# A two-layer decoder step on one core: score products of 64 rows in two banks, normalized queries stored once, down rows of the experts requested early, norms and vector work reordered

## The reference: what is computed

```
def layer_forward(x, c, ...):
    sh1, sc1, gt1, sh2, sc2, gt2 = split(silu(c) @ w_ada + b_ada, 6)
    h = rms_norm(x, g_mix) * (1 + sc1) + sh1
    q, k, v, u, g = in_proj(h, w_in, ...)     # q, k: 4 heads x 2 maps x 64, rms-normed per map
    o = attend(q, k, v, lam)                  # softmax(map 0) - lam * softmax(map 1), times v
    o = rms_norm(o, subln) * (1 - lambda_init)
    y_pool = pool_mix(u, ...)                 # trailing windows 2, 4, 8, 16
    merged = g0 * (o @ w_branch[:512]) + g1 * (y_pool @ w_branch[512:])
    x = x + gt1 * (merged @ w_out)
    h2 = rms_norm(x, g_ffn) * (1 + sc2) + sh2
    f = swiglu(h2, ...)       if layer == 0   # d_ff 2816
        moe_swiglu(h2, ...)   if layer == 1   # top 2 of 8 experts, each 1024 x 3584 gate, up, down
    return x + gt2 * f
```

## Time and profile before

| | |
|---|---|
| time, median of 3 | 1641.35 us (1641.23 to 1641.9) |
| the profiled execution | 1645.29 us, its span 1643.6 us |
| PE busy | 1601.4 us, 97% of the span |
| DVE, ACT, POOL busy | 414.5, 150.2, 69.6 us |
| moved by DMA | 535.14 MB, mean 326 GB/s |
| granted TensorE clock, mean | 0.996 |

### The profile page before, as it was taken

One profiled execution on the slowest core, in us unless ns is written; L12 is line 12 of the kernel. 1 busy time (PEld: TensorE's weight loads), 2 busy tenths in 40 slices (PEclk: granted clock), 3 DMA queues, 4 the chain that ended last, 5 costly groups with the idle time before them and its releaser, 6 DMA issues.

```text
span 1643.6 us, 34513 instructions
## 1 busy us (share of the span) xinstructions
PE 1601.4 (97%) x15756; PEld 1002.9 (61%) x15756; DVE 414.5 (25%) x877; ACT 150.2 (9%) x364; POOL 69.6 (4%) x118
## 2 busy tenths in 40 slices
PE   7999999999999999999999999999999999999997
PEld 3778887888886888863444444444554555555544
DVE  4468353101103794441111001100110011011132
ACT  2102301000002112130000000000000000000000
POOL 1111500000000010001000000000000000000010
PEclk8999999999999999999999999999999999999999
DMA  9998878564348877348999999999999999999995
GB/s 364 365 374 303 284 255 258 163 201 145 123 159 285 272 256 230 128 134 343 404 418 418 404 417 404 418 418 404 418 416 404 412 393 418 418 399 418 411 386 186
DMA packets 188920, 535.14 MB, mean 326 GB/s; under 512 B 13047, under 2 KB 113189, under 8 KB 175970
## 3 DMA queue, kind: packets, MB, share of 16 engines
q1 hardware_dynamic: 173298, 497.20, 79.9%
q0 software_dynamic: 8768, 28.96, 5.0%
q10 hardware_dynamic: 6704, 6.72, 1.3%
HBM read 517.47 MB, written 15.82 MB: 324 GB/s over the span
## 4 chain that ended last, share of the span: by engine, by line
PE 81%; DMA 12%; DVE 4%; SPq 1%; issue 1%; ACT 0%; POOL 0%; DVEq 0%
PE bank L1465 30%; PE bank L1486 14%; PE bank L1109 11%; PE bank L1022 10%; DMA ring<-in_w_exp_up 9%; PE bank L1322 5%; PE bank L1298 3%; PE bank L1286 2%; PE bank L1030 1%; DMA ring<-in_w_ada 1%; DVE inv L1922 1%; DMA w_route<-in_w_router 1%; PE bank L1273 1%; SPq L591 1%; PE bank L1124 1%
## 5 line engine op out<-in xcount | busy, mean ns | idle before, releaser
L1465 PE MATMUL bank<-ring,area 128*32 128x448 f32 x3072 | 302.9, 539 | 3.5 <-DMA ring<-in_w_exp_up 3.2
L1465 PE MATMUL bank<-ring,xT 128*32 128x448 f32 x3072 | 301.7, 539 | 3.6 <-DMA ring<-in_w_exp_up 3.4
L1109 PE MATMUL bank<-hT,ring 128*128 128x264 f32 x1024 | 239.3, 389 | 0.8 <-ACT hT L814 0.8
L1486 PE MATMUL bank<-area 128*32 128x256 f32 x3840 | 227.8, 379 | 1.2 <-issue 1.0
L1109 PEld LDWEIGHTS bank<-hT,ring 128*128 128x128 f32 x1024 | 193.4, 191 | 36.4 <-issue 4.5
L1465 PEld LDWEIGHTS bank<-ring,area 128*32 128x32 f32 x3072 | 109.8, 110 | 165.0 <-issue 157.8
L1465 PEld LDWEIGHTS bank<-ring,xT 128*32 128x32 f32 x3072 | 111.0, 110 | 162.6 <-issue 154.7
L1486 PEld LDWEIGHTS bank<-area 128*32 128x32 f32 x3840 | 139.2, 110 | 100.0 <-issue 44.3
L496 DVE TENSOR_TENSOR area<-bank,area 128x448 f32<-128x448 f32 x48 | 45.9, 956 | 577.5 <-ACT area L981 577.5
L1022 PE MATMUL bank<-hT,ring 128*128 128x264 f32 x704 | 157.4, 386 | 0.0
L1022 PEld LDWEIGHTS bank<-hT,ring 128*128 128x128 f32 x704 | 133.7, 190 | 23.2 <-issue 0.4
(11 more groups left out here) (314 smaller groups left out, 882.1 us busy)
## 6 DMA issues: line engine op xcount, KB each, us to landing
ring<-in_w_exp_gate SPq DMA_DIRECT2D x128, 896.0 KB, 18.2
ring<-in_w_exp_up SPq DMA_DIRECT2D x128, 896.0 KB, 20.0
area<-in_w_exp_down SPq DMA_DIRECT2D x64, 1024.0 KB, 18.3
ring<-in_w_ada SPq DMA_DIRECT2D x96, 512.0 KB, 10.4
ring<-in_w_in SPq DMA_DIRECT2D x32, 1024.0 KB, 12.5
ring<-in_w_exp_down SPq DMA_DIRECT2D x32, 1024.0 KB
area<-in_w_exp_down SPq DMA_DIRECT2D x32, 512.0 KB
ring<-in_w_ff_gate SPq DMA_DIRECT2D x22, 512.0 KB, 7.3
```

The lines of the kernel that those rows point to most:

```text
L1109: mm = pe.matmul(bank[b][:, 0:T], w[:, c, :], hT[:, c, :], start=(c == 0), stop=(c == DC - 1))
L1465: mm = pe.matmul(bank[t + 3 * half][32 * g:32 * g + 32, 0:SLICE], tokens[:, t, 32 * r:32 * r + 32], w[half][:, SLICE * g:SLICE * (g + 1)], ...
L1486: mm = pe.matmul(bank[6 + t // 2][32 * q:32 * q + 32, (t % 2) * S:(t % 2 + 1) * S], FFN["actT"][:, m % 2, t, 32 * i:32 * i + 32], wide(at) ...
```

## The change

1. **Scores.** The queries are stored once (`qn`); the product of map m runs over the 64 rows of that map alone and writes bank 4 + m. One DVE instruction per query head in `norm_qk` takes the place of three, and the four memsets of `qz` go. A score now fills both banks, so `score(n)` waits until DVE has read score n - 1 (before: n - 2). The values move by two z pages (`V_AT`).
2. **Norms.** DVE scales chunk 0 of the prompt tokens first, then does the three instructions for the samples, then chunks 1 to 7. PE waits for `samples_scaled` besides.
3. **Modulation.** Three pages of layer 1 are used before `sums(1)`; three more before `sums(2)` and one behind, which before came between the z pages of layer 1 (`later_ada`).
4. **State transposes** at z 6 and 8 instead of 3 and 5; `late_vectors` (lambda, the last modulation read) before the second `past_scores` instead of behind it.
5. **Early down rows.** Rows 2 to 6 of turn 0 are requested ahead of the pages of step 2 of turn 0, rows 0 and 1 in step 6 of turn 0. Rows 7 to 13 are then requested in steps 0 to 3 of turn 1 instead of 4 to 7.

```diff
-        V_AT = (27, 29)
-        STATE_AT = (3, 5)
+        V_AT = (29, 31)
+        STATE_AT = (6, 8)
+        FIRST_DOWN = DOWN_PAGES[1:4]
-            first, last = ((16, 48), (32, 40))[l]
+            first, last = ((16, 48), (36, 40))[l]
-                for n in range(16, 32):
+                for n in (*range(16, 24), *range(32, 35), *range(24, 32), 35):
                     yield ada_page(l, n)
@@ sync
             for r in range(DC // 2):
+                if r == 2:
+                    for i, n in FIRST_DOWN:
+                        down_rows_in(0, i, n)
                 gate_up_pages(0, r)
...
                         if m < TURNS and (m or r >= DC // 2):
                             gate_up_pages(m, r)
-                        if m:
+                        if m == 0 and r == DC - 2:
+                            down_rows_in(0, *DOWN_PAGES[0])
+                        if m == 1 and r < len(FIRST_DOWN):
+                            down_rows_in(0, *DOWN_PAGES[4 + r])
+                        if m == 1 and r == len(FIRST_DOWN):
+                            down_rows_in(0, *DOWN_PAGES[7])
+                        if m > 1:
                             i, n = DOWN_PAGES[r]
                             down_rows_in(m - 1, i, n)
@@ tensor
-                    if n >= 2:
-                        pe.wait_ge(s.score_out, 8 * l + n - 1)
+                    if n:
+                        pe.wait_ge(s.score_out, 8 * l + n)
                     for m in range(2):
-                        mm = pe.matmul(bank[4 + n % 2][:, m * S:m * S + w], ATT["qz"][:, m, h, i * P:(i + 1) * P],
-                                       ATT["kT"][:, h, 0:w], start=True, stop=True)
+                        r = slice(m * HD, (m + 1) * HD)
+                        mm = pe.matmul(bank[4 + m][:, 0:w], ATT["qn"][r, h, i * P:(i + 1) * P],
+                                       ATT["kT"][r, h, 0:w], start=True, stop=True)
...
+                if l == 0:
+                    for n in range(3):
+                        modulation(1, n, 7)
                 sums(2 * l + 1)
                 if l == 0:
-                    for n in range(16):
+                    for n in range(3, 16):
                         modulation(1, n, 7)
@@ vector, norm
-                step(dve.tensor_tensor(hT[:, :, S:T], xT[:, :, S:T], inv[...], ALU.mult))
-                step(dve.tensor_tensor(hT[:, :, S:T], hT[:, :, S:T], gain[:, :, 1:NC], ALU.mult))
-                step(dve.tensor_tensor(hT[:, :, S:T], hT[:, :, S:T], sh[:, :, 1:NC], ALU.add))
                 for c in range(DC):
                     dve.scalar_tensor_tensor(out=hT[:, c, 0:S], ...).then_inc(s.h_scaled, 1)
+                    if c == 0:
+                        (the same three, the last with .then_inc(s.h_scaled, 1))
@@ vector, norm_qk, i < QC
-                    (two scalar_tensor_tensor into qz, one into q_s)
+                    dve.scalar_tensor_tensor(out=ATT["qn"][:, i, :], in0=q, scalar=g, in1=inv[:, :], ...)
@@ vector
                     if i == 15:
                         past_scores(0)
+                        late_vectors()
                         past_scores(1)
```

More of the change, by code:

```diff
@@ L146, in sem @@
             return ctx.enter_context(nc.semaphore(name))
-        bank = [ctx.enter_context(nc.psum_tensor(f"bank{i}", [P, 512], F32)) for i in range(8)]
+        banks = ctx.enter_context(nc.psum_tensor("bank", [P, 8, 512], F32))
+        bank = [banks[:, i, :] for i in range(8)]
         cst = sb("cst", [P, CW])
@@ L641, in _ @@
                     sp.wait_ge(page_in[eslot[2 * k]], landed[eslot[2 * k]] + 16)
+                for i, _ in FIRST_DOWN:
+                    sp.wait_ge(page_in[eslot[2 * DC + i]], landed[eslot[2 * DC + i]] + 16)
                 with sp.Fori(0, E) as e:
@@ L1017, in column @@
             def column(out, w, x, ready=None):
+                if ready is not None:
+                    pe.wait_ge(s.h_scaled, samples_scaled(ready // DC))
                 for c in range(DC):
@@ L1086, in _ @@
                         modulation(1, n, 0)
+                    for n in range(32, 35):
+                        modulation(1, n, 1)
                     sums(2)
@@ L1089, in _ @@
                         modulation(1, n, 0)
+                    modulation(1, 35, 1)
                 def z(i):
@@ L1106, in z @@
                     for c in range(DC):
+                        if i == 0 and c == 0:
+                            pe.wait_ge(s.h_scaled, samples_scaled(2 * l))
                         if i == 0:
@@ L1362, in _ @@
             pe.wait_ge(s.tok_out, 6)
+            pe.wait_ge(s.h_scaled, samples_scaled(2 * LAYERS - 1))
             for c in range(4):
@@ L1572, in _ @@
                                 if j == 0:
-                                    pe.wait_ge(page_in[at], n * 16 + (landed[at] + 16))
+                                    pe.wait_ge(page_in[at], n * 16 + (landed[at] + (32 if i in [first for first, _ in FIRST_DOWN] else 16)))
                                 mm = pe.matmul(bank[4 + j % 4][:, 0:T], wide(at)[:, j * P:(j + 1) * P], FFN["act"][:, i, :],
@@ L1849, in _, with late_vectors @@
                 spare = ATT["prob"].rearrange("p a b -> p (a b)")[:, 0:512]
+                def late_vectors():
+                    if l == 0:
+                        dve.wait_ge(s.lam_exp, 1)
+                        for n in range(LAYERS):
+                            step(dve.tensor_tensor(neglam[:, n:n + 1], lam[:, 2 * n + 1:2 * n + 2], lam[:, 2 * n:2 * n + 1], ALU.subtract))
+                            step(dve.tensor_scalar(neglam[:, n:n + 1], neglam[:, n:n + 1], -LAM_INIT[n], None, ALU.add))
+                    step(dve.scalar_tensor_tensor(out=comb_m[:, :], in0=const("comb_b", 64), scalar=neglam[0:64, l:l + 1],
+                                                  in1=const("comb_a", 64), op0=ALU.mult, op1=ALU.add))
+                    if l:
+                        read_mod(l, 1, 32, 39, spare[:, 0:S], 8).then_inc(s.mod_out, 1)
+                    else:
+                        read_mod(l, 1, 32, 47, spare).then_inc(s.mod_out, 1)
                 for i in range(ZC):
@@ L1853, in _ @@
                         read_state(STATE_AT.index(i))
-                    if l == 0 and i == 4:
+                    if l == 0 and i == 7:
                         lam_sums()
@@ L1874, in _ @@
                         past_scores(0)
+                        late_vectors()
                         past_scores(1)
-                if l == 0:
-                    dve.wait_ge(s.lam_exp, 1)
-                    for n in range(LAYERS):
-                        step(dve.tensor_tensor(neglam[:, n:n + 1], lam[:, 2 * n + 1:2 * n + 2], lam[:, 2 * n:2 * n + 1], ALU.subtract))
-                        step(dve.tensor_scalar(neglam[:, n:n + 1], neglam[:, n:n + 1], -LAM_INIT[n], None, ALU.add))
-                step(dve.scalar_tensor_tensor(out=comb_m[:, :], in0=const("comb_b", 64), scalar=neglam[0:64, l:l + 1],
-                                              in1=const("comb_a", 64), op0=ALU.mult, op1=ALU.add))
-                if l:
-                    read_mod(l, 1, 32, 39, spare[:, 0:S], 8).then_inc(s.mod_out, 1)
-                else:
-                    read_mod(l, 1, 32, 47, spare).then_inc(s.mod_out, 1)
                 past_scores(2); read_v(0); past_scores(3); read_v(1); past_scores(4); past_scores(5); read_new()
```

33 lines of the change are left out of this document (14 added, 19 removed).

## The result

The changed kernel takes 1688.85 us (median of 4, 1685.36 to 1690.14) against 1641.29 (4 runs, 1639.89 to 1641.9): a ratio of 1.0283, 95% interval 1.0264 to 1.0302, or 47.6 us more. The forecast was 33.3 more; the time lies inside the range of 1661 to 1690, near its end. The profiled execution took 1689.0 us, that of before 1645.29.

A forecast was written before the change was run, and what follows sets the result against it. In the experts PE and DMA limits were taken to lie side by side, memory ending last; before them PE bounds. Memory +33.0 and clock +7.5 give +40.5, less 7.2 gained earlier: +33.3 on 1641.35, 1674.6 us; range 1661 to 1690.

The forecast's parts named there:

- The holes: Turn 1 of the experts: PE runs dry four times behind rows 7 to 13, 36.7 us in all.
- The memory's account: Experts: the memory stream falls behind, less the 8.8 us of rows already on chip; +33.0 us without the clock.
- PE's account: Experts: PE is 36.7 us late and wins back at most 12.6 of later waits, leaving 24.
- The clock: Bursts behind turn 1's holes start at half clock: 2.5 us each, three delay requests, 7.5 us.
- Rival (a): Turn 1 of the experts: no clock loss, bursts run at 2.4 GHz; 1667.1 us, chance 0.24.
- (b): Turn 1 of the experts: bursts run at half clock throughout, 20.0 us more; 1687.2 us, chance 0.16.
- 7.2 us gained, bounds 1 and 11: Ahead of the experts: sum of all gains from PE's shortened or removed waits, 7.2 us.
- Four pages moved around `sums(2)`: 1.8 gained: Around `sums(2)`: modulation pages fill holes of 1.29 us before and 0.8 behind; 1.8 us gained.
- in layer 1 ... I take 0.9: Layer 1: vectors ahead of the second `past_scores` remove PE's wait for `mod`; 0.9 us gained, nothing in layer 0.
- I take +1.0 for both layers together, bounds -3 and +5: Scores: row groups run at once, wide saving 0.5 us, narrow half; switch to 64-row products unpriced; 1.0 us gained.
- State transposes and `sums(1)`: Ahead of the experts: z pages cover the router's transfer wait, 2.2 us; modulation pages fill the `sums(1)` hole, 1.3.
- The norms' order: Reordered norm: chunk 0 at most 0.4 us earlier for PE, chunk 1 as late as before; 0.

The follow-up runs named there:

- holes_filled_by_8us: Kernel before with only the change's down-row order, plus 18 unused PE products ahead of each of turn 1's steps 1 to 4: 1676.33 us.
- one_hole: Kernel before with rows 2 to 6 early and only rows 7 and 8 ahead of turn 1's step 1, rows 9 to 13 at steps 5 to 7: 1649.45 us.
- early_rows_alone: Kernel before with down rows 2 to 6 early, rows 0 and 1 in turn 0's step 6, rows 7 to 13 where they were: 1634.73 us.
- scores_alone: Kernel before with the change's scores part alone, without the moved values: 1643.31 us.
- rows_all_back: Changed kernel with all down rows, layer 1's four moved modulation pages and the late vectors put back as before: 1641.49 us.
- kept_parts: Changed kernel with scores, layer 1's four modulation pages and rows 7 to 13 as before, late vectors early in layer 0 alone: 1632.91 us.
- rows_back_in_turn1: Changed kernel with rows 7 to 13 requested in steps 4 to 7 of turn 1 again, rows 2 to 6 still early: 1641.36 us.
- rows_back_mod_back: Changed kernel with rows 7 to 13 and layer 1's four moved modulation pages put back as before: 1636.85 us.
- mod_and_vectors_back: Changed kernel with rows 7 to 13, layer 1's four moved modulation pages and the late vectors put back as before: 1636.92 us.
- rows_back_vectors_back: Changed kernel with rows 7 to 13 put back and the late vectors behind the second past_scores again in both layers: 1640.48 us.

## Why the prediction was right or wrong

**The holes: right, in place, number and size.** Forecast 3 x 9.5 + 8.2 = 36.7 us; measured 9.38 + 9.31 + 9.22 + 8.55 = 36.5. SP's pause is 24 us as foretold.

**The memory's account: right.** It gave +33.0 without the clock. The experts of holes_filled_by_8us take 922.67 - 890.43 = 32.2 more. PE's account (win back up to 12.6) was the wrong model, as one_hole shows: what offsets the holes is the bytes brought early, 7.1 us in the experts of early_rows_alone (3.9 by the medians), near the 8.8 that the account took off.

**The clock: the mechanism right, the size right in the trace.** Forecast 2.5 us for each, three of them counting, 7.5. The bursts took 1.5, 2.7, 1.6 and 2.1 longer than 4.7, and filling the holes took 6.7 from the experts of the traced executions, but only 3.0 from the medians, so the term's share in the total is not settled. The rule of the Trainium skill ("TensorE: Matmul & The Clock Gate", the section on HAM oscillation), that short bursts between waits for DMA start cold each time, agrees with the four bursts. Rival (a) is out as a mechanism, since the clock did fall, and (b) too, since no burst took twice its time. Holes and clock together: forecast +40.5, measured 929.67 - 890.43 = +39.2.

**Before the experts: wrong.** The step that failed is "7.2 us gained, bounds 1 and 11"; layer 1 lost 8.8 (222.69 - 213.86). By its terms:

- "Four pages moved around `sums(2)`: 1.8 gained": a loss of 4.3 to 4.5 us. I counted the holes that the pages fill and not the ring. Sixteen modulation pages and the z pair fill its 18 buffers; twenty don't leave room for the pair.
- "in layer 1 ... I take 0.9" for the late vectors: a loss of 0.6 and 1.8 in the traces. DVE behind them waits for keys.
- "I take +1.0 for both layers together, bounds -3 and +5" for the scores: a loss of 2.1 by the medians. In the trace of scores_alone it is 2.5 in layer 1 and 1.2 between the first score of layer 0 and `sums(1)` (119.64, before 118.48), 3.7 and so outside the bounds. The step that failed is the price of the switch to 64-row products and back: a z page right behind a score takes 0.20 us more from start to start, nearly the 0.24 that a wide score saves (0.5 was taken) and more than the 0.02 of a narrow one (0.25 was taken). The Trainium skill names a drain at such a switch ("TensorEngine Tiling (Array Packing)", Key Properties). The trace agrees with one, though no run separates whether it is all of the 0.20. On top comes a later `mod` by 0.36 and, in scores_alone, the clock behind it, 1.7. rows_all_back has the same scores and wait without the fall of the clock, and its layer 1 still takes 1.8 more than before.
- State transposes and `sums(1)`, 2.2 and 1.3: both waits are gone in the trace. The second is worth about 1.1 there: from the first score of layer 0 to `sums(2)` kept_parts takes 365.64, before 366.72. But the wait for the router's transfer varies between executions of the same instructions (2.2 to 2.4 us in five traces, 0.69 in holes_filled_by_8us, with `sums(2)` 5 us earlier there), so of the 3.9 us by which the changed kernel was ahead at layer 1, 1.7 stood there already at its second group of z pages (46.22, 47.90 before). Two pairs of medians show both terms together, with the norms' order and the values' place in them (and in the first the early vectors of layer 0): kept_parts takes 1.8 less than early_rows_alone, rows_all_back 1.8 less than scores_alone. That is half of the 3.5 forecast, within noise of about 2.
- The norms' order, 0: between `sums(3)` and the experts 0.1.

In the traces layer 1's 8.8 add up, each as a difference of two neighbours: 4.3 the pages (rows_back_in_turn1 to rows_back_mod_back), 1.8 the vectors (to mod_and_vectors_back), 1.7 what is left of the change there, the scores above all, and 1.05 that the changed kernel and rows_back_in_turn1 differ by with the same program. So a term near 1 us is not told from chance by one trace.

**The total** came out 14.3 above the forecast: 15.6 ahead of the experts (a gain of 7.2 forecast, 47.6 - 39.2 = 8.4 lost) less 1.3 in the experts. Of the 15.6 the two traces show 12.0, since the experts begin 4.8 late; the rest is that the profiled execution of before was 4.0 above its own median, so that the two executions differ by 43.7 us, 3.9 less than the medians. That the time still fell inside the range is luck: the range reached up to 1690 for the sake of rival (b), whose 1687.2 is the nearest of the numbers and whose mechanism did not occur.

## What to carry to other kernels

A queue in order makes each waiting request a gate for all behind it: before moving a request forward, ask when its buffer comes free and who wants what stands behind it. A move that fills an idle gap with pages must also be counted in the ring's buffers, here 18, for the pages that follow them. And a product that takes fewer microseconds by its own row is priced from its start to the start of what follows: here the z page behind it took back what a score saved. Where PE then waits for another engine, ask when that engine gets there, not when PE does.

## What the hardware showed unexpectedly

The length of a wait of about 2 us did not decide on the clock behind it. At the same place, the wait for `mod` in layer 1, 1.79 us of idle left the 32 records behind it at 7.29 us (the kernel before, kept_parts), while 2.14 and 2.15 made them 8.97 in rows_back_vectors_back and scores_alone. But in mod_and_vectors_back and rows_all_back the wait was 2.14 as well and the records stayed at 7.29, in the first of them:

```profile
585.14 0.66 PE L1133 MATMUL bank<-cst,area 128*128 128x128 f32 x4 [2.14 <-DVE mod L1696]
585.63 7.29 PE L1128 MATMUL bank<-hT,ring 128*128 128x264 f32 x32
```

The wait of 2.20 at 57.93 was followed by z pages at their usual 3.72 too. What tells the two outcomes apart no run here shows; a wait of this size may cost up to 1.7 us more than itself. A longer one, of 3.33 at 1587.37 in one_hole, was followed by a burst of 6.41 instead of 4.72.

Two products of 64 rows in different banks overlap more than two of 128: 0.42 and 0.63 us from the start of the four records to the next instruction's, where 128-row products took 0.44 and 0.87. A z page right behind them took 0.20 us more from start to start, which by the busy time of its row looks like 0.1 (3.83 instead of 3.72 or 3.73), since the spans of neighbours overlap.
